# Modulation, first norm and mixer of a two-layer decoder trunk: the order of the first loads and sums, and three reorderings in each layer

## What is computed

```
mod = ada_b + silu(c) @ ada_w                          # 6*1024 columns: shift, scale, gate, twice
h = rms_norm(x) * norm1_g * (1 + scale1) + shift1
x = x + gate1 * ([attention | mLSTM](h @ w_in) @ w_out)
h = rms_norm(x) * norm2_g * (1 + scale2) + shift2
x = x + gate2 * ((silu(causal_conv(h @ up_a)) * (h @ up_v)) @ down)
```

## Time and profile before

| | |
|---|---|
| median of 3 runs | 1462.16 us (1461.49 to 1464.21) |
| profiled execution, its span | 1462.0 us, 1460.3 us |
| PE busy | 1414.4 us (97%) |
| DVE, ACT, POOL busy | 636.1, 512.7, 650.3 us |
| chain that ended last | PE 81%, issue 5%, DVE 5%, POOL 3%, ACT 2% |
| 16 DMA engines, 6 to 38 us | 90% and more, about 400 GB/s |

### The profile page before, as it was taken

One profiled execution on the slowest core, in us unless ns is written; L12 is line 12 of the kernel. 1 busy time (PEld: TensorE's weight loads), 2 busy tenths in 40 slices (PEclk: granted clock), 3 DMA queues, 4 the chain that ended last, 5 costly groups with the idle time before them and its releaser, 6 DMA issues.

```text
span 1460.3 us, 17608 instructions
## 1 busy us (share of the span) xinstructions
PE 1414.4 (97%) x7099; PEld 1168.3 (80%) x7099; DVE 636.1 (44%) x1067; ACT 512.7 (35%) x679; POOL 650.3 (45%) x298
## 2 busy tenths in 40 slices
PE   5799999999999999999999999999999999999998
PEld 5688887777788888888878888787778888888886
DVE  5746456757554554443231464675432221211131
ACT  4222444552433333321132234445433333333112
POOL 0344325234554554555633432444264554554562
PEclk8899999999999999999999999999999999999999
DMA  9633210043266666664342321100022333322231
GB/s 365 227 118 97 69 59 30 1 144 116 87 185 193 195 177 191 193 210 162 109 116 64 129 72 58 59 1 1 30 87 87 107 95 87 113 89 92 92 105 58
DMA packets 181974, 163.20 MB, mean 112 GB/s; under 512 B 16037, under 2 KB 147589, under 8 KB 181893
## 3 DMA queue, kind: packets, MB, share of 16 engines
q1 hardware_dynamic: 180724, 161.83, 35.2%
q10 hardware_dynamic: 1169, 0.25, 0.1%
HBM read 159.96 MB, written 2.10 MB: 111 GB/s over the span
## 4 chain that ended last, share of the span: by engine, by line
PE 81%; issue 5%; DVE 5%; POOL 3%; ACT 2%; POOLq 1%; DMA 1%; DVEq 0%; ACTq 0%; SPq 0%
PE psum L1589 19%; PE psum L1591 19%; PE psum L1590 19%; PE psum L1621 4%; PE psum L1622 4%; PE psum L1624 3%; PE psum L1907 2%; POOL w_lo L561 2%; PE psum L1630 1%; PE psum L1772 1%; DVE psum L1076 1%; ACT w_hi L728 1%; PE psum L1569 1%; PE psum L1893 1%; PE psum L1958 1%
## 5 line engine op out<-in xcount | busy, mean ns | idle before, releaser
L561 POOL TENSOR_TENSOR w_lo<-w_raw,w_hi 128x2048 fp32r<-128x2048 f32 x76 | 351.1, 4619 | 468.4 <-ACT w_hi L728 467.4
L728 ACT ACTIVATE w_hi<-w_raw 128x2048 fp32r<-128x2048 f32 (+2 forms) x104 | 192.9, 1855 | 581.3 <-PE psum L1591 467.1
L1589 PE MATMUL psum<-h_hi,w_hi 128*128 128x512 f32 x928 | 366.5, 395 | 2.1 <-POOL w_lo L561 1.1
L1591 PE MATMUL psum<-h_hi,w_lo 128*128 128x512 f32 x928 | 361.6, 390 | 0.0
L1590 PE MATMUL psum<-h_lo,w_hi 128*128 128x512 f32 x928 | 361.2, 389 | 0.0
L1589 PEld LDWEIGHTS psum<-h_hi,w_hi 128*128 128x128 f32 x928 | 174.4, 188 | 38.3 <-POOL w_lo L561 1.8
L1591 PEld LDWEIGHTS psum<-h_hi,w_lo 128*128 128x128 f32 x928 | 174.2, 188 | 36.8
L1590 PEld LDWEIGHTS psum<-h_lo,w_hi 128*128 128x128 f32 x928 | 174.4, 188 | 34.8
L566 POOL TENSOR_TENSOR w_lo<-w_raw,w_hi 128x1792 fp32r<-128x1792 f32 (+2 forms) x28 | 112.4, 4013 | 131.0 <-ACT w_hi L728 131.0
L1483 DVE SCALAR_TENSOR_TENSOR fy<-psum,par,fy 128x511 f32<-128x511 f32 x44 | 33.0, 750 | 269.2 <-ACT fy L935 269.2
L1589 PE MATMUL psum<-hid_hi,w_hi 128*128 128x512 f32 x352 | 137.8, 392 | 0.0
(11 more groups left out here) (270 smaller groups left out, 1899.3 us busy)
## 6 DMA issues: line engine op xcount, KB each, us to landing
w_raw<-in_ffn_up SPq DMA_DIRECT2D x88, 512.0 KB, 4.9
a_raw<-in_ada_w SPq DMA_DIRECT2D x56, 512.0 KB, 4.7
w_raw<-in_w_in SPq DMA_DIRECT2D x48, 512.0 KB, 4.5
w_raw<-in_ffn_down SPq DMA_DIRECT2D x32, 512.0 KB, 4.3
w_raw<-in_w_out SPq DMA_DIRECT2D x16, 512.0 KB, 4.3
a_raw<-in_ada_w SPq DMA_DIRECT2D x7, 1024.0 KB, 5.4
w_raw<-in_ffn_down SPq DMA_DIRECT2D x16, 384.0 KB, 3.1
a_tok<-in_ada_w SPq DMA_DIRECT2D x5, 1024.0 KB, 7.0
```

Of the source, the lines that this page charges most:

```text
L561: g.tensor_tensor(w_lo[:, slot_of(l, u), :], w_raw[:, slot_of(l, u), :], w_hi[:, u % HI, :].bitcast(F32), ALU.subtract).then_inc(s_lo, 1)
L728: s.activation(w_hi[:, u % HI, 0:n], w_raw[:, r, 0:n], ACT.Copy).then_inc(s_hi, 1)
L1589: m(ps, l_hi, r_hi, start=first, stop=False)
L1591: return m(ps, l_lo, r_hi, start=False, stop=last)
```

## The change

It moves work at the program's start, in the mixer of both layers, and in the row maxima.

Start: the loads go 4, 5, 0, 1, unit 0, 6, 2, 3, 7 (in two parts), units 1 and 2. silu(c) is made first, from c alone (a semaphore and a transpose of its own). The first norm is made in two halves of 4 chunks: DVE sums halves 4, 5 and 1, PE half 0 (16 matmuls of one column), `first_modulation(0)`, and then chunks 0 to 3 run; between them DVE does halves 2 and 7, while halves 6 and 3 are scaled on ACT (`early_scaled`) and added up on POOL (`early_part`). PE sums them after the third chunk of unit 0, and `first_modulation(1)` releases chunks 4 to 7. Unit 0 is split in two parts on ACT and POOL. `gate_b` goes to ACT's queue, the sine tables behind unit 2 on ACT, the load of unit 3 ahead of those of halves 12 and 13. PE gets ten 128x512 matmuls that compute nothing (`keep_clock`).

Each layer: maxima in the fourth mLSTM unit go one or two at a time, one of them between a k chunk's two banks; `sources(0)` goes behind `values` of step 18; chunks 0 to 3 of the mixer are turned ahead of and amid the last head's values, chunks 4 and 5 a k chunk earlier, and the square root of three heads is taken ahead of the fourth.

```diff
--- before.py
+++ after.py
...
-            for i in (2, 3, 0, 1, 4, 5, 6, 7):
...
+            for i in (4, 5, 0, 1):
+                sp.dma_start(*early_rows(i, 0, 4)).then_inc(s_e[i], 16)
...
+                    if l == 0 and u == 0:
+                        for i in (6, 2, 3):
+                            sp.dma_start(*early_rows(i, 0, 4)).then_inc(s_e[i], 16)
+                        sp.dma_start(*early_rows(EARLY - 1, 0, 2)).then_inc(s_e[EARLY - 1], 16)
+                        sp.dma_start(*early_rows(EARLY - 1, 2, 4)).then_inc(s_e7b, 16)
...
+                    if j == EARLY + ARING:
+                        load_w_in(l, RAW)
                     load_ada(j)
...
-            low(0, 0)
+            def early_part(n, j):
+                cols = a_early[j].rearrange("p (k n) -> p k n", k=KD // 2)
+                for kk in range(1, KD // 2):
+                    pool.wait_ge(s_scaled, n * KD // 2 + kk + 1)
+                    g.tensor_tensor(part[:, n, :], part[:, n, :] if kk > 1 else cols[:, 0, :], cols[:, kk, :], ALU.add)
+                    last = pool.drain()
+                last.then_inc(s_aused, 1)
+                if n == 1:
+                    pool.wait_ge(s_asum, 3)
+                    g.tensor_tensor(part[:, n, :], part[:, n, :], asum0[:, 0, :], ALU.add)
+                pool.drain().then_inc(s_part, 1)
+            for i in range(2):
...
+                pool.wait_ge(s_hi if i else s_hi0, 1)
+                g.tensor_tensor(w_lo[:, slot_of(0, 0), cols], w_raw[:, slot_of(0, 0), cols],
+                                w_hi[:, 0, cols].bitcast(F32), ALU.subtract).then_inc(s_lo if i else s_lo0, 1)
+            early_part(0, 6)
+            early_part(1, 3)
...
+            def early_scaled(j):
+                cols = a_early[j].rearrange("p (k n) -> p k n", k=KD // 2)
+                act.wait_ge(s_e[j], 16)
+                for kk in range(KD // 2):
+                    k = j % 2 * (KD // 2) + kk
+                    s.activation(cols[:, kk, :], cols[:, kk, :], ACT.Identity, bias=0.0,
+                                 scale=cact[:, k:k + 1]).then_inc(s_scaled, 1)
...
+                    if c8 == 2 and not chunks:
+                        early_scaled(3)
                     if c8 == 3 and not chunks:
                         high(l, u)
...
+            for i in range(2):
...
+                s.activation(w_hi[:, 0, cols], w_raw[:, r, cols], ACT.Copy).then_inc(s_hi if i else s_hi0, 1)
+            early_scaled(6)
...
-                head_squares(MH - 2)
                 for c8 in range(KD // 2):
                     mixer_high(c8)
+                head_squares(MH - 2)
+                s.activation(ssq2[:, :, NH:NH + MH - 1], ssq[:, :, NH:NH + MH - 1], ACT.Sqrt, bias=eps[:, 0:1],
+                             scale=1.0 / MD).then_inc(s_rt2, 1)
...
+                if n == 0:
+                    scaled(0)
+                    scaled(1)
+                    remainder(0)
+                    second_half(2, (0, 1), None, None)
+                    scaled(2)
+                    remainder(1)
+                    second_half(2, (2, 3), bank[6], asum0[:, 0, :])
+                    remainder(2)
+                    dve.wait_ge(s_part, 1)
+                    second_half(7, range(KD // 2), part[:, 0, :], asum0[:, 1, :])
+                    scaled(3)
+                    remainder(3)
+                    first_modulation(1)
...
+            def first_modulation(half):
+                dve.wait_ge(s_ag, 2 * half + 2)
+                c = slice(half * KD // 2, (half + 1) * KD // 2)
+                mod2, sum2, par2 = (t.rearrange("p (a c) -> p a c", c=KD)[:, :, c]
+                                    for t in (mod[:, 0:2 * KD], bank[6][:, 0:2 * KD], par[:, AB:AB + 2 * KD]))
+                v.tensor_tensor(mod2, sum2, par2, ALU.add)
+                dve.drain()
+                v.scalar_tensor_tensor(out=am[:, 0, c], in0=mod2[:, 1, :], scalar=1.0,
+                                       in1=par[:, N1:N1 + KD][:, c], op0=ALU.add, op1=ALU.mult)
+                if half == 0:
+                    v.tensor_tensor(mod[:, c], mod[:, c], bank[6][:, 2 * KD:2 * KD + KD // 2], ALU.add)
+                last = dve.drain()
+                if half:
+                    last.then_inc(s_mod, 1)
...
+            dve.wait_ge(s_cact, 1)
+            early_half(4, bank[2], False)
+            parameter_columns()
+            early_half(5, bank[2], True, asum0[:, 0, :]).then_inc(s_asum, 1)
             rstd(0)
...
+            early_half(1, bank[2], False, asum0[:, 1, :]).then_inc(s_asum, 1)
+            dve.wait_ge(s_gb, 16)
+            first_modulation(0)
             for l in range(L):
...
+                mixer_low(0)
+                mixer_low(1)
                 head_out(MH - 1, 0, 1)
                 head_out(MH - 1, 1, 2)
...
+                mixer_low(2)
+                mixer_low(3)
+                for i, heads in enumerate((range(MH - 1), range(MH - 1, MH))):
+                    roots = ssq2[:, :, NH + heads[0]:NH + heads[-1] + 1]
+                    dve.wait_ge(s_rt2, l * 3 + 2 + i)
+                    v.reciprocal(roots, roots)
+                    dve.drain()
+                    for h in heads:
+                        o3 = mixt[:, :, T + h * MD:T + (h + 1) * MD]
+                        v.tensor_tensor(o3, o3, ssq2[:, :, NH + h:NH + h + 1].broadcast_to([P, TT, MD]), ALU.mult)\
+                            .then_inc(s_mixm, 1)
...
+                        if e == 0 and middle is not None:
+                            middle(kk)
...
+            pe.wait_ge(s_e[0], 16)
+            for i in range(4):
+                for k in range(KD // 2):
+                    at = k * T + i * P
+                    last = m(bank[6][:, 2 * KD + i:2 * KD + i + 1], a_early[0][:, at:at + P], cact[:, k:k + 1],
+                             start=k == 0, stop=k == KD // 2 - 1)
+                if i == 0:
+                    pe.wait_ge(s_xu, KD)
+                keep_clock(1, 0)
+            pe.drain().then_inc(s_aused, 1)
+            early_sums(1, 2, asum0[:, 0, :])
             spread(0)
...
+            early_sums(2, 0, asum0[:, 1, :])
+            keep_clock(6, 0)
...
-                ada_at_step = {(1, 3): 4, (2, 1): 5, (3, 1): 6, (U_OUT + 1, 3): 7, (U_OUT + 2, 2): 8} if l == 0 else {}
+                ada_at_step = {(2, 0): 4, (2, 3): 5, (3, 2): 6, (U_OUT + 1, 3): 7, (U_OUT + 2, 2): 8} if l == 0 else {}
                 def beside_ada(u):
                     def between(kk):
                         if (u, kk) in ada_at_step:
                             ada_turns(ada_at_step[u, kk])
+                        if l == 0 and (u, kk) == (0, 2):
+                            pe.wait_ge(s_part, 2)
+                            early_sums(4, 1, part[:, 1, :])
+                            early_sums(4, 3, asum0[:, 1, :])
...
-                        for n in ((), (), (), (0, 1, 2), (3, 4, 5), (6, 7, 8), (9, 10), (11,))[kk]:
+                        for n in ((), (), (), (0, 1), (3, 4), (6, 7), (9,), (11,))[kk]:
                             maxima(n)
+                def amid_mqk(kk):
+                    if kk >= 4:
+                        maxima((2, 5, 8, 10)[kk - 4])
...
-                    if z >= NZ - 2:
-                        sources(z - NZ + 2)
+                    if z == NZ - 1:
+                        sources(0)
+                        sources(1)
                     values(z)
...
+                pe.wait_ge(s_mWS, ends - 2)
+                mixed_chunk(0)
+                mixed_chunk(1)
+                pe.wait_ge(s_mev, l * 8 + 2 * MH - 3)
+                token_values(MH - 1, 0)
+                token_values(MH - 1, 1)
+                pe.wait_ge(s_mWS, ends - 1)
+                mixed_chunk(2)
+                mixed_chunk(3)
+                pe.wait_ge(s_mev, l * 8 + 2 * MH - 2)
+                token_values(MH - 1, 2)
+                pe.wait_ge(s_mWS, ends)
+                token_values(MH - 1, 3)
...
+                        if kk == KD // 2 - 1:
+                            mixed_chunk(KD // 2)
+                            mixed_chunk(KD // 2 + 1)
                         if kk == KD // 2:
-                            for c8 in range(KD // 2, KD):
-                                mixed_chunk(c8)
+                            mixed_chunk(KD // 2 + 2)
+                            mixed_chunk(KD // 2 + 3)
```

More of the change, by code:

```diff
@@ L1036, in finish @@
+                for c8 in range(0 if n else KD // 2, KD + 1):
+                    if c8 < KD:
+                        scaled(c8)
+                    if c8 >= 1 and (n or c8 > KD // 2):
+                        remainder(c8 - 1)
             def finish(c8):
@@ new lines, in early_half, with second_half @@
+            def early_half(j, acc, more, out=None):
+                dve.wait_ge(s_e[j], 16)
+                for kk in range(KD // 2):
+                    last = early_step(j, kk, acc, acc if kk or more else None, out if kk == KD // 2 - 1 else None)
+                return last
```

(9 more changed lines are left out.)

282 lines of the change are left out of this document (132 added, 150 removed).

## The result

| | before | after |
|---|---|---|
| median (lowest to highest) | 1461.87 us (1461.49 to 1464.21, 4 runs) | 1439.15 us (1438.71 to 1439.54, 4 runs) |
| profiled execution, its span | 1462.0, 1460.3 us | 1439.54, 1437.8 us |
| PE busy | 1414.4 us | 1407.8 us |

The ratio is 0.9842, with a 95% interval of 0.983 to 0.9854: 22.7 us less, where 18.6 were forecast.

A forecast was written before the change was run, and what follows sets the result against it. PE bounds the kernel: 46 us of preparation, then 1414 us of products. Start 12.1, clock -1.1, unit 3 0.8, score tile 1.2, maxima 2.5, mixer's end 3.1: 18.6 off 1462.0, so 1443 us; range 1437 to 1451 (8 in 10).

The forecast's parts named there:

- The start: Program start up to weight unit 1: it begins at 46.7 instead of 58.78, 12.1 us earlier, less 1.1 for PE's clock.
- The lock: First norm: DVE's `am`, with two SBUF inputs, waits for POOL's low part until 29.6; first product 29.9, without it 28.4.
- The clock: PE at the start: a fall to 1.2 GHz at 26 costs under 1 us; one between 39 and 43.7 takes 1.1.
- The second fall: PE's clock falling between about 39 and 43.7: sums cost 1.0 more, chunk 3 another 1.5; half taken, 1.1 us.
- Unit 3: Fourth weight unit: its load moves ahead of halves 12 and 13, some 7 us earlier, so PE's 0.83 us wait is won.
- Score tile: First score tile behind the values of step 18: its 0.64 us wait goes, 0.6 a layer, 1.2 in all.
- Maxima: Row maxima in smaller groups: 1.6 us a layer less four interruptions at 0.1, net 1.2, 2.5 in all.
- Mixer's end: Last score tile to second turning: 13.8 us becomes 12.3 (work 11.9, four switches at 0.1); 1.55 a layer, 3.1 in all.
- Hand-overs at half a microsecond more: First rival, at the start: dearer links and unit 2's late low part lose 5 to 8 us, 1448 to 1454; 0.20 with third.
- No lock: Second rival, at the start: POOL does not hold `am` off and PE stays warm, 1436 to 1440 us; chance 0.14.
- Only the front counts: Third rival: mixer's end and maxima give 1 us instead of 5.6, so 1448; chance 0.20 together with the first rival.
- Slower: Rival: PE stays at 1.2 GHz over the first units, each chunk 1.5 to 2.4 us more, up to 1482; chance 0.03.

## Why the prediction was right, and where its terms were not

- **What bounds the kernel** was read rightly: the span is the start plus products, and what was won at the start is still won at the end (11.6 at unit 1, 12.7 before the maxima), given the load of unit 3.
- **The start** (forecast 11.0, measured 11.6 at unit 1) comes out by steps that were partly wrong and made up for each other. The lock was there and cost 1.1 us, but with POOL's first add and not with the low part: the low part was done when `am` came at 29.15, but the add had begun at 29.10, 0.05 us before it. That it waited for POOL although it is four columns wide is read from its ends: 30.39 against the add's 30.37, and, without the bf16 products, 29.15 against the low part's 29.13. By the Trainium skill's rule (SBUF — State Buffer, SBUF: two separate sides) these are waits for the whole instruction; the traces agree, as 1.24 us against 0.16 with a PSUM input, or 0.16 without POOL's adds. The 0.6 for half 7's first step was not paid (0.75 us), by luck: the step began at 38.14, and POOL had a gap from 38.26 to 38.43; with `am` from PSUM it was (1.10).
- **The clock** was priced at the wrong fall. The first, near 26.4, has no term in the sum, and was said to cost less than 1 us, "since PE waits for chunk 2 anyway". It made the sums 1.71 us instead of about 1.0, which is 0.7 of the 1.4 us by which `mod` (28.90) is later than the forecast's 27.5. And PE did not wait for chunk 2, nor for anything between 32.24 and 42.58: its products at 1.2 GHz until 36.6 made the second sums begin 1.2 us after DVE was ready (41.37). In the two profiles whose clock was back at 31.6, PE reached the sums first and stood for 1.12 and 0.93 us, and they began at 41.06 and 41.37. The second fall did not come in the kernel after, which gave back the 1.1 that was taken off for it.
- **Unit 3** is the term whose size was right and whose meaning was not. As a sum over the whole change 0.83 is about right (0.8 to 1.5 measured), and it was costed from the wait of before. What failed is the step "so 0.83 is won": with the front 11 us earlier, that wait would have been 6.9 us and a fallen clock, and the moved load is what keeps 8 to 9 us of the front's gain. The prediction checked the loads of units 1 and 2 against the new times and not that of unit 3 where it stood.
- **Score tile**: 1.2 forecast, 1.2 alone on the chip, 1.4 to 1.6 in the traces.
- **Maxima**: 2.5 forecast, 3.1 alone, 3.2 in the traces. The upper end was the right one: a switch between products and a maximum is free, so the four switches at 0.1 per layer were not to be paid.
- **Mixer's end** is the term of the sum that was mis-sized: 3.1 forecast, 4.7 alone, 5.4 in the traces. "Work stays 11.9" took every busy row as work. The row of 2.10 us at 332.32 in the earlier trace rows held a wait: its last transposes need the fourth head, and DVE's timeline of before has the four multiplications ending at 333.71:

```profile
331.21 2.50 DVE L1464 TENSOR_TENSOR mixt<-mixt,ssq 128x512 f32<-128x512 f32 x4
333.68 2.73 DVE L1417 SCALAR_TENSOR_TENSOR h_lo<-psum,par,h_hi 128x512 fp32r<-128x512 f32 x4
```

  After, the last of them ends at 315.48, ahead of the last eight transposes at 315.96:

```profile
312.73 1.89 DVE L1578 TENSOR_TENSOR mixt<-mixt,ssq 128x512 f32<-128x512 f32 x3
...
314.79 0.69 DVE L1578 TENSOR_TENSOR mixt<-mixt,ssq 128x512 f32<-128x512 f32 x1
```

  The 1.15 us a layer between the 12.3 forecast and the 11.16 measured, by starts of rows: 16 transposes took 334.49 - 332.32 = 2.17 before and take two times 0.88 (305.59 to 306.47) after, 0.4 less, which is the wait. About half of it was inside the row (2.10 us, where the same sixteen took 1.91 at 324.43 and with chunks 4 to 7 together), and half behind it without a bracket: the product needs the low part of chunk 4, which DVE began only at 333.68, behind the multiplications. The other 16 took 326.34 - 324.43 = 1.91 before, 0.15 more than after; the last head's values 2.34 (322.09 to 324.43), now 0.67 + 1.48 = 2.15, 0.2 less; and the four switches at 0.1 are free, 0.4.
- **The rivals.** Hand-overs at half a microsecond more did not show. "No lock" fell, though its time (1436 to 1440) held: it is the forecast's 18.6 plus the mixer's 2.3, the maxima's 0.7, 0.6 of the start and 0.2 to 0.4 of the score tile that make 1439. "Only the front counts" fell, and turned over: the front alone counts for little. "Slower" did not occur in the change, but first products at 1.2 GHz are seen in each of the three variants that let PE stand for 6 us or more.

## What to carry to other kernels

When a change makes the start earlier, ask of every load behind it whether it still arrives in time where it stands: a load that was 0.8 us late before is 7 us late after, and a part measured alone can be worth an eighth of what it is worth beside another (1.2 us against about 10). Where PE waits and then finds its clock down, count both; keeping it fed with real products (the channel halves) was worth 11 us where the first product came 13 us earlier. A row that groups instructions counts waits between them as busy: compare it with the same count of the same instruction elsewhere before calling it work.
